# Keys and values with x as the moving operand, and three smaller reorderings, in a two-layer streaming-encoder trunk

## What is computed

```python
h = rms_norm(x, norm_g)                 # y = x * rsqrt(mean(x*x) + EPS), times norm_g
proj = h @ w_in                         # one projection for everything below
(q, k, v, z_a, p_in, z_b, u, v_sgu, z_c, glu_a, glu_b, z_d, merge) = split(proj)
q = apply_rope(rms_norm(q, q_norm_g))   # 8 heads of 64; k: 2 heads, v: 2 heads
k = apply_rope(rms_norm(k, k_norm_g))
o_a = window_attention(q, k, v, sinks)
o_c = u * (sgu_w per group @ layer_norm(v_sgu) + sgu_b)   # spatial gating
...                                     # branches B and D, gates, merge, w_out
return x + mixed @ w_out
```

## Time and profile before

| | us |
|---|---|
| median of 3 runs (2036.91 to 2037.66) | 2037.42 |
| the profiled execution | 2038.11 |
| its span in the trace | 2036.2 |
| TensorE busy | 2031.4 |
| VectorE busy | 1347.7 |
| GpSimd busy | 1308.2 |
| ScalarE busy | 883.8 |

### The profile page before, as it was taken

One profiled execution on the slowest core, in us unless ns is written; L12 is line 12 of the kernel. 1 busy time (PEld: TensorE's weight loads), 2 busy tenths in 40 slices (PEclk: granted clock), 3 DMA queues, 4 the chain that ended last, 5 costly groups with the idle time before them and its releaser, 6 DMA issues.

```text
span 2036.2 us, 27175 instructions
## 1 busy us (share of the span) xinstructions
PE 2031.4 (100%) x9592; PEld 1690.7 (83%) x9592; DVE 1347.7 (66%) x1625; ACT 883.8 (43%) x1653; POOL 1308.2 (64%) x980
## 2 busy tenths in 40 slices
PE   9999999999999999999999999999999999999999
PEld 7988888888888888888888888888888888888887
DVE  5986543888878645338869764438888786453384
ACT  6655644343233334324647455443432343443242
POOL 2767555776669667554727675467766797675545
PEclk9999999999999999999999999999999999999999
DMA  7133323313431343313431332223135213434142
GB/s 277 38 94 86 93 92 112 96 52 84 90 72 52 83 83 79 138 52 114 145 90 37 104 94 94 99 89 94 57 78 97 65 57 81 91 73 145 42 135 104
DMA packets 122758, 186.13 MB, mean 91 GB/s; under 512 B 30976, under 2 KB 40320, under 8 KB 122624
## 3 DMA queue, kind: packets, MB, share of 16 engines
q1 hardware_dynamic: 105040, 155.14, 24.8%
q0 software_dynamic: 9216, 16.78, 6.1%
q10 hardware_dynamic: 8368, 12.47, 1.9%
HBM read 141.34 MB, written 41.95 MB: 90 GB/s over the span
## 4 chain that ended last, share of the span: by engine, by line
PE 97%; DVE 1%; DMA 1%; SPq 0%; ACT 0%; issue 0%; DVEq 0%; POOL 0%; ACTq 0%; POOLq 0%
PE acc L795 88%; PE aux L906 2%; PE acc L885 1%; PE aux L885 1%; PE aux L978 1%; PE acc L999 1%; PE aux L946 1%; PE aux L1014 1%; PE aux L986 1%; PE acc L856 1%; PE aux L856 1%; DVE flo L1683 0%; DMA x<-x 0%; DMA xrow<-x_rows 0%; PE aux L960 0%
## 5 line engine op out<-in xcount | busy, mean ns | idle before, releaser
L795 PE MATMUL acc<-fhi,whi 128*128 128x512 f32 x2140 | 834.9, 390 | 0.2 <-DVE x L1680 0.2
L718 POOL TENSOR_TENSOR wlo<-raw,whi 128x512 fp32r<-128x512 f32 x392 | 551.5, 1409 | 437.2 <-ACT whi L1112 436.4
L795 PE MATMUL acc<-fhi,wlo 128*128 128x512 f32 x2140 | 832.2, 389 | 0.0
L795 PE MATMUL acc<-flo,whi 128*128 128x512 f32 x2140 | 832.0, 389 | 0.0
L795 PEld LDWEIGHTS acc<-fhi,whi 128*128 128x128 f32 x2140 | 401.9, 188 | 83.6 <-issue 1.4
L795 PEld LDWEIGHTS acc<-fhi,wlo 128*128 128x128 f32 x2140 | 401.8, 188 | 83.5
L795 PEld LDWEIGHTS acc<-flo,whi 128*128 128x128 f32 x2140 | 401.9, 188 | 81.8
L718 POOL TENSOR_TENSOR wlo<-wsum,whi 128x512 fp32r<-128x512 f32 x222 | 320.6, 1444 | 195.4 <-ACT whi L1112 194.7
L1112 ACT ACTIVATE whi<-raw 128x512 fp32r<-128x512 f32 x392 | 245.7, 628 | 364.6 <-PE acc L795 321.1
L1687 DVE SCALAR_TENSOR_TENSOR aux<-conv,allp,aux 128x1024 f32<-128x1024 f32 x232 | 299.0, 1289 | 20.4 <-issue 0.9
L1112 ACT ACTIVATE whi<-wsum 128x512 fp32r<-128x512 f32 x222 | 139.8, 630 | 220.1 <-PE acc L795 164.3
(11 more groups left out here) (252 smaller groups left out, 2206.3 us busy)
## 6 DMA issues: line engine op xcount, KB each, us to landing
raw<-wstream SPq DMA_DIRECT2D x392, 256.0 KB, 2.8
md<-prev POOLq DMA_DIRECT2D x64, 256.0 KB, 4.3
x<-x SPq DMA_DIRECT2D x32, 256.0 KB, 4.8
md<-prev SPq DMA_DIRECT2D x32, 256.0 KB, 3.2
out<-x ACTq DMA_DIRECT2D x31, 256.0 KB, 2.1
mx<-md SPq DMA_DIRECT2D x24, 256.0 KB, 5.0
xrow<-x_rows SPq DMA_DIRECT2D x8, 512.0 KB, 6.7
qs<-qd SPq DMA_DIRECT2D x32, 128.0 KB, 2.8
```

The lines of the kernel that those rows point to most:

```text
L718: nc.gpsimd.tensor_tensor(wlo[:, f % SLOTS, :], src, whi[:, f % SLOTS, :].bitcast(F32), ALU.subtract).then_inc(lo_made, 1)
L795: mm = nc.tensor.matmul(dst, w, m[:, kt0 + k, cols], start=first and k == 0 and n == 0, stop=last and k == UK - 1 and n == 2, skip_group_c ...
```

## The change

KV's operands change places: 128 columns of weights are stationary, 512 tokens of x move, and K^T and V^T come out with channels on the partitions, K in `aux[:, 0]`, V in `aux[:, 1]`. K is copied out by VectorE with one multiplication by `spreads` (`scale_k`). V is copied plain by ScalarE (`copy_v`, to `vraw`), turned by eight transposes ahead of p7, and copied out with the norms per token (`take_v`). F6's highs are copied to PSUM as B22's are, and Q's p1 waits for F6's second rest. F4's rests and the scaling of K stand ahead of all of the gate's statistics. In layer 0 the last two norm rows and the root are taken behind tile 4 of x in place of tile 3.

```diff
@@ TensorE, keys_values @@
-                    for tile in range(TT):
-                        if k == 0 and tile % 4 == 0:
-                            pe.wait_ge(vs_taken, 8 * L + 2 + tile // 2)
-                        for e in range(2):
-                            kx = 2 * k + e
-                            s = X_SLOT[kx // UK, tile // 4]
-                            at = slice(tile % 4 * P, (tile % 4 + 1) * P)
-                            w_at = slice(e * 2 * P, (e + 1) * 2 * P)
-                            for m, (h, w) in enumerate(((fhi, whi), (flo, whi), (fhi, wlo))):
-                                mm = nc.tensor.matmul(kv_bank(tile), h[s][:, kx % UK, at], w[:, slot, w_at],
-                                                      start=kx == 0 and m == 0 and tile % 2 == 0,
-                                                      stop=kx == KT - 1 and m == 2, skip_group_check=True)
+                    for kx in (2 * k, 2 * k + 1):
+                        for c in range(2):
+                            if kx == 0:
+                                pe.wait_ge(vs_taken, 8 * L + 2 + 2 * c)
+                            at = (kx % 2 * 2 + c) * P
+                            wh, wl = whi[:, slot, at:at + P], wlo[:, slot, at:at + P]
+                            for t in range(2):
+                                s = X_SLOT[kx // UK, t]
+                                for m, (w, h) in enumerate(((wh, fhi), (wh, flo), (wl, fhi))):
+                                    mm = nc.tensor.matmul(aux[:, c, t * HALF:(t + 1) * HALF], w, h[s][:, kx % UK, :],
+                                                          start=kx == 0 and m == 0, stop=kx == KT - 1 and m == 2)
@@ TensorE, row_sums, turn, head_sums, pair @@
-                pe.wait_ge(kv_taken, 16 * (L + 1))
+                pe.wait_ge(v_taken, TT * (L + 1))
-            def turn_k(L):
+            def turn_v(L):
-                pe.wait_ge(kv_taken, 16 * (L + 1))
+                pe.wait_ge(v_copied, L + 1)
-                    mm = nc.tensor.transpose(aux[:, 0, t * P:(t + 1) * P], krow[:, t, :], ident[:])
+                    mm = nc.tensor.transpose(aux[:, 1, t * P:(t + 1) * P], vraw[:, t * P:(t + 1) * P], ident[:])
-                    pe.wait_ge(k_copied, L + 1)
+                    pe.wait_ge(k_scaled, L + 1)
-                            pe.wait_ge(form_ready, form_n(L, RESTS, "B22", 1))
+                            pe.wait_ge(form_ready, form_n(L, RESTS, "F6", 1))
-                pair(L, "Q", 0, {"p3": lambda L=L: turn_k(L), "p4": lambda L=L: row_sums(L)})
+                pair(L, "Q", 0, {"p7": lambda L=L: turn_v(L), "p4": lambda L=L: row_sums(L)})
@@ ScalarE @@
+            def copy_f6(L, n):
+
+                act.wait_ge(form_hi, form_n(L, HIGHS, "F6", n))
+                act.wait_ge(form_ready, form_n(L, RESTS, "B22", n))
+                copy(acc[:, 1 - n, :], fhi[S_F6][:, 2 * n:2 * n + 2, :].rearrange("p k t -> p (k t)").bitcast(F32)
+                     ).then_inc(f6_copied, 1)
-            def take_kv(L, c):
+            def copy_v(L):
+                act.wait_ge(step_done, stepped(L, "KV", 3))
+                copy(vraw[:], aux[:, 1, :]).then_inc(v_copied, 1)
+
+            def take_v(L):
-                act.wait_ge(step_done, stepped(L, "KV", 3))
+                act.wait_ge(turned, L + 1)
-                    nc.scalar.activation((krow, vt)[c][:, t, :], kv_bank(t)[:, c * P:(c + 1) * P], ACT.Copy,
-                                         scale=rms[:, t:t + 1]).then_inc(kv_taken, 1)
-
-            def take_turned_k(L):
-                act.wait_ge(turned, L + 1)
-                copy(kraw[:], aux[:, 0, :]).then_inc(k_copied, 1)
+                    nc.scalar.activation(vt[:, t, :], aux[:, 1, t * P:(t + 1) * P], ACT.Copy,
+                                         scale=rms[:, t:t + 1]).then_inc(v_taken, 1)
-                for t in ROWS_AT[k]:
+                for t in ROWS_AT[k] if k < 3 else ROWS_AT[3] if k == 4 else ():
-                if k == 3:
+                if k == 4:
                     rms_stage(0)
                     store_norms(0)
-                form_rounded(L, ("F6", 0), ("F6", 1), ("F5", 0), ("F5", 1))
+                for n in range(2):
+                    form_rounded(L, ("F6", n))
+                    copy_f6(L, n)
+                form_rounded(L, ("F5", 0), ("F5", 1))
-                take_kv(L, 0)
+                copy_v(L)
-                    "p1": lambda: take_kv(L, 1), "p5": lambda: form_rounded(L, ("F4", 0), ("F4", 1)),
-                    "p2": lambda: (take_turned_k(L), square_a(L, 0), square_high(L, 0))})
+                    "p5": lambda: form_rounded(L, ("F4", 0), ("F4", 1)), "p7": lambda: take_v(L),
+                    "p2": lambda: (square_a(L, 0), square_high(L, 0))})
@@ VectorE @@
+            def rest_f6(L):
+                for n in range(2):
+                    at = slice(2 * n, 2 * n + 2)
+                    dve.wait_ge(f6_copied, 2 * L + n + 1)
+                    sub(flo[S_F6][:, at, :].rearrange("p k t -> p (k t)"), x22[:, at, :].rearrange("p k t -> p (k t)"),
+                        acc[:, 1 - n, :]).then_inc(form_ready, 1)
+            def scale_k(L):
+                dve.wait_ge(step_done, stepped(L, "KV", 3))
+                mul(kraw[:], aux[:, 0, :], spreads[:]).then_inc(k_scaled, 1)
-                if k == 4:
+                if k == 5:
                     norms(0)
-                form_rest(L, ("F6", 0), ("F6", 1), ("F5", 0), ("F5", 1))
+                rest_f6(L)
+                form_rest(L, ("F5", 0), ("F5", 1))
-                dve.wait_ge(vs_taken, 8 * L + 8)
-                gate_stats(range(2))
                 sum_22(L, "Q", 0, qhi[0][:, HALF:SEQ])
                 form_rest(L, ("F4", 0), ("F4", 1))
-                gate_stats(range(2, 5))
+                scale_k(L)
+                dve.wait_ge(vs_taken, 8 * L + 8)
+                gate_stats(range(5))
```

## The result

The changed kernel takes 2041.37 us, the median of 21 runs (2039.12 to 2043.29); the kernel before took 2037.42 in the 21 runs beside them. The ratio is 1.0019, interval 1.0013 to 1.0025: about 3.9 us slower, and outside the range I had given. Both are needed.

The account below looks back on a forecast made before the run. TensorE bounds the kernel (busy 2031.4 of 2036.2 us), with VectorE nearly as full in layer 0. Layer 0's +1.7 and layer 1's -1.26 gave +0.4 us: 2038.5 profiled, 2037.8 median; range -1.0 to +1.9 us, chance 0.50.

Parts of the forecast that it names:

- Keys and values: KV stage on TensorE, both layers: 96 matmuls of 512 columns take 21.8 us for 23.0, gaining 1.26 us per layer.
- rival C: KV stage: the wide loop isn't faster; +1.4 to +1.7 us, 2039.0; chance 0.03.
- Norm rows: Layer 0, tiles 4 and 5 of x: TensorE gains 0.8 us, VectorE's scaling of x begins 1.75 us later.
- slack of 1.46: Layer 0: VectorE's list ended at 108.12, TensorE wanted its last item at 109.58, so 1.46 us lateness is free.
- F6 through PSUM: F6's highs and rests before Q's p1: VectorE's wait for ScalarE's copy loses 0.9 us in layer 0, 0.3 in layer 1.
- Gate statistics and K: VectorE's list: statistics' sum unchanged, F4's rests 1.3 us earlier, K's multiplication adds 1.17 us.
- Rival B: Layer 0: VectorE's lateness grows as its list runs into GpSimd's sums; at 5 us delay +2.3, 2039.7; chance 0.20.
- Layer 0: VectorE's list ends 3.85 us late, 2.4 past use; between ends 3.0 and about 0.3, the middle taken: 1.7 us slower.
- Layer 1: VectorE's slack of 3.68 us leaves 0.9 after all terms, so the 1.26 us gain stays whole.
- from span to median: Whole kernel: the median lay 0.7 us below the profiled execution, so forecast 2038.5 became a median of 2037.8.

Follow-up runs that it names:

- b_norms_only: Kernel before with only the norm rows, root and store moved behind tile 4 of x; 2038.99 us, ratio 1.0012.
- a_norms_back: Changed kernel with the norm rows, root and store put back behind tile 3 of x; 2039.99 us, ratio 1.0008.
- a_order: Changed kernel with norm rows and F6's rests put back as before, new order and K's multiplication kept; 2036.97 us, ratio 0.9997.
- b_order_only: Kernel before with only F4's rests put ahead of all the gate's statistics; 2037.38 us, ratio 1.0000.
- g_less: Changed kernel with three of GpSimd's subtractions in layer 0 (Q's p2, p3, p4) cut to 64 of 512 columns; 2039.39 us, ratio 1.0009.
- a_again: Changed kernel run and profiled once more without any edit; 2041.15 us, ratio 1.0020 to the kernel before.
- a_kv_only: Changed kernel with norm rows, F6's rests and first gate statistics as before, leaving the wide loop and new ways of K and V; 2038.54 us, ratio 1.0003.
- a_f6_back: Changed kernel with F6's copies removed and its rests made from SBUF again; 2038.85 us, ratio 1.0006.
- b_late: Kernel before with three unused 1024-column subtractions added to VectorE's list in layer 0; 2045.14 us (five runs), ratio 1.0039.

## Why the prediction was wrong

The step that failed is the path through VectorE's list, in both layers: I let the list keep its length but for two terms, took its lateness at the end as the sum of those, and set it against a slack. The runs show that the list grows on its way, by 1.1 us for each operation of 1024 columns from SBUF that comes to lie beside one of GpSimd's, that F6's copies cost it twice what I had counted, and that the slack was smaller. Each term in turn:

**Keys and values, right.** 21.76 us in the changed kernel for 23.03, in both layers; forecast 21.8. The pace of 0.227 us held, and rival C is out.

**Norm rows, the size of the delay right, what it costs wrong.** Tile 4 began at 29.01 (forecast 28.4) and tile 5 at 34.45 (34.4); keys and values began 0.79 earlier (0.8). The scaling began 0.77 later in the profiled execution, not at 41. But this start moves by a microsecond either way from run to run. Over the seven profiles with the rows moved it lies at 39.43 to 41.41, mean 40.6, over the ten others at 37.55 to 39.61, mean 38.8: 1.8 later, and I had said 1.75. Taken alone it cost 1.7 us net (b_norms_only). What failed is the slack of 1.46. It covers only a delay that keeps its length, and this one grew by 2.25 on the way.

**F6 through PSUM, mis-sized.** I counted one wait of 0.9 in layer 0 and 0.3 in layer 1. The changed kernel shows 0.93 and 0.82, and 1.02. On ScalarE the rounding of the second part stands behind the copy of the first (68.23, 69.32, 70.29 and 71.36 are the starts of rounding, copy, rounding, copy), which I did not put into the sum. The list grew by 49.72 - 47.90 = 1.8 (a_norms_back against a_order). Measured: 1.7 us alone, and 3.0 between those two.

The Trainium skill (SBUF — State Buffer, SBUF: two separate sides) calls the ports that VectorE and GpSimd share an exclusive lock that blocks the other for a whole instruction. The rows agree more fully than I used them: a rest with two SBUF operands takes 1.21 or up to 2.32 us, one with a PSUM operand 1.21, and GpSimd's operation 1.29 or 2.27. By that rule F6 was to gain 0.8; it did not, because F6's rests ran where GpSimd was idle (1.21 and 1.23 us before), and those that follow were pushed to where it works.

**Gate statistics and K, right.** K's multiplication takes 1.21 (forecast 1.17) and was worth 1.0 and 1.6 to 1.8 us when left out, though the part of the list that it stands in grew by nothing in layer 0. The order alone changed nothing (b_order_only).

**Left out of the sum altogether: GpSimd's gaps.** Of the ScalarE copies that moved away from the end of keys and values and from p1 I asked only whether TensorE would want them. I had written that rests were long "only where GpSimd ran beside them", named up to 0.4 us for each of some 20 operations as a bound, and then did not ask what the change does to GpSimd. The price of one meeting is 1.1 us, not 0.4, and one more of them came with the wide loop and the new ways of K and V alone: the list of a_order is 1.2 us longer with the same instructions. g_less takes 2.8 away, two to three of them. Rival B came nearest, with the right mechanism ("its list now also runs into GpSimd's sums") and a chance of 0.20.

**Layer 0: +1.7 forecast**, +2.45 in the quick execution and +4.3 in a_again. My terms as they stood gave 2.4 before I moved to the middle of the ends, and that this is the quick execution's number is luck: I had 1.75 + 0.9 + 1.2 less 1.46, the trace has 0.77 for the start, 1.75 for F6, 1.2 for durations, 0.2 less behind `v`, and a slack of 1.1. **Layer 1: -1.26 forecast**, -0.7 and +0.4. I had said that waits in layer 1 would show its slack misjudged, and they do. With the distance of 3.0 this can be worked out. Layer 0: the last item begins 3.56 and 5.43 us later than before, less the true slack of 1.1, makes 2.5 and 4.3. Layer 1: the list from F5's form on (1073.59 to 1122.02, in a_again 1075.41 to 1125.01; before 46.08) grew by 2.35 and 3.5; of the slack 3.2 - 1.26 = 1.9 is left; 0.45 and 1.6 late, so the 1.26 became -0.8 and +0.3. Both agree with the timeline to about 0.1. I had taken the slacks as 1.46 and 3.68, from the end of VectorE's last item to the mix, and had overlooked that TensorE asks VectorE 9.2 us ahead of the mix, at the head sums.

**The sum in medians.** Kernel before 2037.4; wide loop and new ways of K and V +1.0 (a_kv_only), order -1.6 (a_order against it), F6 +3.0 (a_norms_back against a_order), norm rows +1.9 (a_f6_back against a_order): 2041.7, measured 2041.2 to 2041.4. (The kernel before beside a_order was 0.4 lower than beside the others; with that taken out, order is -1.2, F6 +2.6, norm rows +1.5, and the sum 2041.3. Each of these differences is uncertain by 1 us or more, so that they add up is a check of the whole and not of each.)

**Also wrong: from span to median.** I carried the 0.7 us by which the profiled run of the kernel before lay above its median over to the changed one. But its scaling of x happened to start at 39.61, the latest of the ten profiles without the rows moved, and the changed kernel's at 40.38, a little ahead of the mean of its seven. A slack read from one execution is that of this execution.

**Still open.** What holes in TensorE's work bring the clock down. It fell behind waits of 1.9, 2.2, 2.9 and 3.4 us, and stayed up behind 2.4 (changed kernel), 2.5 (b_norms_only) and 2.9 (b_late, p3). Of the two groups of a_f6_back, some 2.3 us apart, the clock explains 0.9 on the path; I take the rest for the start of the list and its meetings with GpSimd, but that was not tried. Nor was it tried apart which closed GpSimd's gaps, the copies taken from ScalarE or the earlier end of keys and values; the timeline before has both.

## What to carry to other kernels

Where VectorE and GpSimd share the memory ports, look at the least and the greatest duration of one operation and not at the mean: the price of VectorE's list is the short time plus so many meetings, here at 1.1 us each, and every edit that makes GpSimd denser, or shifts VectorE against it, changes their number. So when work is taken off a third engine, follow it through whom it feeds: ScalarE's relief became GpSimd's, and that was VectorE's loss. And a slack of a microsecond on such a list is none, since a delay grows before it arrives (at `v` 0.9 had become 3.2 in b_norms_only, and 3.6 had become 6.5 in b_late).

## What the hardware showed beyond that

GpSimd's subtraction of 64 columns took 1.30 us beside VectorE's rests, the same as 512 columns take where nothing disturbs them (1.29). I read this as the length of VectorE's operation (1.2 to 1.3) counting there, and not its own; no run tested it. It cost VectorE less all the same: 2.8 us, two to three meetings.

TensorE's granted clock fell to its lower level behind some holes of 1.9 us and more, and 36 matmuls then took 10.06 us for 8.16, or 12 took 4.5 for 3.0. Where another wait followed, this cost nothing; where none did, 0.9 us.
